# An expert's first and third matrix: one unit each with products of 256 columns, in place of halves of both with products of 512

## The reference

```python
def run(args):
    e, xb = args
    h = jax.nn.silu(xb @ w1[e]) * (xb @ w3[e])
    return h @ w2[e]
```

## Time and profile before

| | us |
|---|---|
| median of 3 runs | 2414.84 |
| lowest, highest | 2403.18, 2431.26 |
| the profiled execution | 2418.18 |
| its span, first to last instruction | 2416.5 |
| TensorE busy | 2115.9 (88%) |
| VectorE busy | 1528.7 (63%) |
| ScalarE busy | 1182.5 (49%) |
| mean granted TensorE clock | 0.871 |

### The profile page before, as it was taken

The page is one execution under the profiler, slowest core; times in us unless marked ns, Lnnn a source line. Parts: engine busy times, 40 slices in busy tenths (PEclk is TensorE's granted clock), DMA queues, the critical chain, the costliest instruction groups (busy, mean ns, idle before and its releaser), DMA issues.

```text
span 2416.5 us, 27567 instructions
## 1 busy us (share of the span) xinstructions
PE 2115.9 (88%) x9196; PEld 1693.5 (70%) x9196; DVE 1528.7 (63%) x1917; ACT 1182.5 (49%) x1407; POOL 124.9 (5%) x173
## 2 busy tenths in 40 slices
PE   5889989985899999999558899898859999999992
PEld 4776657864787788778447766677648877788871
DVE  4344344236699999999433443524258999999992
ACT  3333232222577777777332332423127777777771
POOL 0000000000010001001000000000000110000110
PEclk9885559997899999999778755899869999999996
DMA  6200022323799999999442000223239999999983
GB/s 223 102 3 0 1 86 72 101 99 122 265 365 362 367 366 369 372 365 365 154 156 104 1 1 1 105 87 114 92 132 341 368 361 369 363 362 368 371 327 119
DMA packets 148804, 501.40 MB, mean 207 GB/s; under 512 B 25312, under 2 KB 25312, under 8 KB 148704
## 3 DMA queue, kind: packets, MB, share of 16 engines
q1 hardware_dynamic: 135984, 460.80, 52.4%
q0 software_dynamic: 12720, 39.33, 4.4%
HBM read 484.35 MB, written 25.17 MB: 211 GB/s over the span
## 4 chain that ended last, share of the span: by engine, by line
PE 78%; DVE 9%; issue 5%; ACT 5%; DMA 2%; SPq 1%; DVEq 0%; POOL 0%; POOLq 0%; ACTq 0%
PE ps L1214 21%; PE ps L1216 20%; PE ps L1215 20%; PE ps L1393 4%; PE ps L1379 3%; PE ps L1351 3%; PE ps L1347 3%; DVE wl L852 1%; ACT wh L583 1%; PE ps L1483 1%; ACT whm L583 1%; PE ps L1442 1%; DVE sel L1129 1%; DMA y<-yrows 1%; PE ps L1455 1%
## 5 line engine op out<-in xcount | busy, mean ns | idle before, releaser
L852 DVE TENSOR_TENSOR wl<-raw,wh 128x2048 fp32r<-128x2048 f32 (+3 forms) x270 | 545.3, 2046 | 300.7 <-ACT wh L583 299.6
L583 ACT ACTIVATE wh<-raw 128x2048 fp32r<-128x2048 f32 (+3 forms) x270 | 455.4, 1718 | 286.9 <-PE ps L1216 277.5
L852 DVE TENSOR_TENSOR wlm<-raw,whm 128x2048 fp32r<-128x2048 f32 x192 | 436.2, 2288 | 52.7 <-ACT whm L583 52.7
L583 ACT ACTIVATE whm<-raw 128x2048 fp32r<-128x2048 f32 x192 | 362.6, 1908 | 0.0
L1214 PE MATMUL ps<-wh,xgh 128*128 128x512 f32 x520 | 212.0, 408 | 1.4 <-issue 1.4
L1216 PE MATMUL ps<-wh,xgl 128*128 128x512 f32 x520 | 207.7, 400 | 0.0
L1214 PE MATMUL ps<-whm,xgh 128*128 128x512 f32 x504 | 205.0, 407 | 2.5 <-DVE xgl L856 2.5
L1215 PE MATMUL ps<-wl,xgh 128*128 128x512 f32 x520 | 207.3, 399 | 0.0
L1216 PE MATMUL ps<-whm,xgl 128*128 128x512 f32 x504 | 197.1, 391 | 0.0
L1215 PE MATMUL ps<-wlm,xgh 128*128 128x512 f32 x504 | 196.7, 390 | 0.0
L767 ACT ACTIVATE hth<-ps 128x256 fp32r<-128x256 f32 x128 | 49.2, 384 | 192.2 <-PE ps L1483 192.2
(11 more groups left out here) (304 smaller groups left out, 3991.9 us busy)
## 6 DMA issues: line engine op xcount, KB each, us to landing
raw<-in_w SPq DMA_DIRECT2D x512, 512.0 KB
raw<-in_w SPq DMA_DIRECT2D x128, 1024.0 KB
raw<-in_w_gate SPq DMA_DIRECT2D x16, 1024.0 KB
x<-xres POOLq DMA_DIRECT2D x4, 2048.0 KB, 8.3
raw<-in_w_out SPq DMA_DIRECT2D x8, 1024.0 KB
raw<-in_w_in SPq DMA_DIRECT2D x8, 800.0 KB
raw<-in_w_oa SPq DMA_DIRECT2D x4, 1024.0 KB
raw<-in_w_ob SPq DMA_DIRECT2D x4, 1024.0 KB
```

The lines of the kernel that those rows point to most:

```text
L583: last = nc.scalar.activation(dst, src, ACT.Copy)
L852: last = V.tensor_tensor(dst, src, hi.bitcast(F32), ALU.subtract)
```

## The change

An up unit holds one whole matrix: half 0 is `w1` of the expert, half 1 is `w3`. SyncE loads it with one DMA of 1 MB, whose run is 8 KB for each partition, and the semaphore is raised by 32 at once. TensorE makes for each of the 8 values of k three products of 256 columns, into columns 0 to 255 (half 0) or 256 to 511 (half 1) of the same bank. As each up unit now reads all of `xgh` and `xgl`, both halves of the next block's tokens are split behind up(7,1), and the first up unit of a block waits for both. The wait of ScalarE for the unit ahead of `rows_hi` goes, as the sigmoid just ahead has the same one.

```diff
@@ load_units (SyncE)
-                            kh = KD // 2
-                            for j, w in enumerate((w1, w3)):
-                                src = w[l].rearrange("e (p k) f -> e p k f", k=KD)
-                                sp.dma_start(dst.rearrange("p (j k f) -> p j k f", j=2, k=kh)[:, j],
-                                             src[bass.ds(ex, 1), :, half * kh:(half + 1) * kh, :]
-                                             .rearrange("o p k f -> (o p) k f")).then_inc(got, 16)
+                            src = (w3 if half else w1)[l].rearrange("e (p k) f -> e p (k f)", k=KD)
+                            sp.dma_start(dst, src[bass.ds(ex, 1)].rearrange("o p n -> (o p) n")).then_inc(got, 32)
@@ act_block, step (ScalarE)
-                        if kind == "up" and e == NE - 1 and prepare:
-                            act.wait_ge(S["unit_used"], r * NU + (n + 1))
-                            rows_hi(b + 1, half)
+                        if kind == "up" and e == NE - 1 and half == 1 and prepare:
+                            rows_hi(b + 1, 0)
+                            rows_hi(b + 1, 1)
@@ dve_block, step (VectorE)
-                        if kind == "up" and e == NE - 1 and prepare:
-                            rows_lo(b + 1, half)
+                        if kind == "up" and e == NE - 1 and half == 1 and prepare:
+                            rows_lo(b + 1, 0)
+                            rows_lo(b + 1, 1)
@@ pe_block, up (TensorE)
                         if e == 0:
-                            pe.wait_ge(S["xgl_done"], b * 2 + (half + 1 + BASE["xgl_done"]))
+                            pe.wait_ge(S["xgl_done"], b * 2 + (2 + BASE["xgl_done"]))
                         if half == 0:
 
                             pe.wait_ge(S["hw_done"], b * (2 * NE) + (2 * (e - 1) + BASE["hw_done"]))
-                        kh = KD // 2
-                        for k in range(kh):
-                            kk = half * kh + k
-                            ww = [w.rearrange("p (j k f) -> p k j f", j=2, k=kh)[:, k]
-                                  for w in (hi_at(n), lo_at(n))]
-                            last = mm3(ps[e % 2][:, :], xgh[:, kk, :], xgl[:, kk, :], *ww, kk == 0, kk == KD - 1)
+                        for k in range(KD):
+                            ww = [w[:, k * FE:(k + 1) * FE] for w in (hi_at(n), lo_at(n))]
+                            last = mm3(ps[e % 2][:, half * FE:(half + 1) * FE], xgh[:, k, :], xgl[:, k, :], *ww,
+                                       k == 0, k == KD - 1)
                         last.then_inc(S["unit_used"], 1)
```

## The result

The changed kernel takes 2454.33 us (median of 16 runs, 2437.1 to 2470.42), the kernel before, run beside it, 2404.31 us (median of 16, 2398.61 to 2432.47). The ratio is 1.0172, 95% interval 1.0136 to 1.0208: slower by 1.7%. It is the ratio of the means of these runs, 2452.3 and 2410.9 us; the medians differ by 50 us, 2.1%. Ratios further down aren't ratios of two medians either, and leave out runs that lie far above the fastest of their kernel. Forecast were 2,455 us and 1.7% slower.

The account below looks back on a forecast made before the run. TensorE's issue of products was taken to bound the kernel. Products +32, turns +7 and layer heads +1.4 made +40 us on the profiled 2,418.2, so 2,458, or 2,455 us for the median, 1.7% slower; range 2,418 to 2,500.

Parts of the forecast that it names:

- The bound: Expert block: TensorE's issue of products sets the 70.19 us; the DMA keeps pace and ScalarE never waits for landed units.
- The products: Up units: 3,072 products of 512 columns become 6,144 of 256, 0.120 us apart in place of 0.2297 per 512: +32 us.
- the line through 384 and 512 columns: Product start distances 0.1765 and 0.2329 us, 0.441 ns a column, extended to give 0.120 us at 256 columns.
- The turn: Between blocks, the first product waits for both rows_lo: 0.5 us at each of 14 turns, +7 us, plus 1.4 at layer heads.
- the 0.1 deducted for a TensorE that comes later: At the block's turn, TensorE arrives 0.12 us later itself, so the 0.60 us delay was counted as 0.5.
- the head of the first stage: At each layer's first block, the first product waits for both rows_lo: +0.7 us, twice, 1.4 us.
- rival 5: Up units: each added weight load stands bare, costing 0.111 us in full, +341 us, 2,764 us in all; chance 0.02.
- 1 (columns alone, 0.115): Up products: the surplus goes with the columns, distance near 0.115 us, 2,423 us, within 1%; chance 0.20.
- 2 (load floor, 0.111): Up products: only the weight-load floor counts, distance 0.111 us, products gain 24 us, 2,399 us; chance 0.08.
- Rival 3: Up products: load and stream collide when equally long, distance 0.13 us or more, 2,516 us at 0.130; chance 0.09.
- rival 4: Up-unit loads: DMA becomes the bound with 8 KB runs; 2,476 us at a rate 5% lower; chance 0.03.

Follow-up runs that it names:

- the products alone: Kernel before with only each up product of 512 columns cut into two of 256, old loads and token-split order kept: 2450.55 us, ratio 1.0187.
- The order alone: Kernel before with only both halves of the next block's token split moved behind up(7,1), first product waiting for both: 2429.8 us, ratio 1.0101.

## Why the prediction was right

**The bound.** TensorE's distances set the block, not the DMA. The 8 KB runs changed the DMA share by 3 points and the block by nothing, and ScalarE's splits had no idle time ahead of them in either kernel.

**The products.** The step was 3,072 x (2 x 0.120 - 0.2297) = +32 us, and the distance of 0.120, read off the line through 384 and 512 columns, was measured. Its last digit is in part luck: both points of the line were of tile wh, the tiles differ by 7 ns at 512 columns and not at 256, and no run here explains the surplus. The term itself was too large. The run with the products alone gave 23.1 us (11.7 and 11.4), 8.5 less, and three things make up most of it. The mean distance of the up products before was nearer to 0.231 than to 0.2297 (92 distances in wh of 0.2333, 89 in whm of 0.2288), as whm units run their first products at the slower distance: 3,072 x 0.0014 = 4.3 us. Two waits for `hw` shrank, as a longer up unit gives VectorE time. Behind up(0,1) the transposes started 0.54 us after the last product had (839.09 to 839.63), 0.31 more than a product of 512 columns takes; in the run alone it is 0.27, 0.15 more than one of 256 takes. And the 0.15 us ahead of the turn went. Together 0.31 a block, 5 us in 16, and the prediction counted it nowhere, though the wait for `hw` stands in the earlier trace rows. In the other direction the down products of whm stood 0.2291 us apart in place of 0.2264, which took 1.9 us.

**The turn.** Forecast 14 x 0.5 + 1.4 = 8.4 us. The order alone cost 10.2 in its stages, 0.61 a block: the 0.60 that the prediction worked out from the length of rows_lo. It can't test the 0.1 deducted for a TensorE that comes later, since its products are the old ones. The changed kernel can, and there the deduction was right: rows_lo began 0.23 us behind the last down product before (897.21 to 897.44) and 0.08 after (744.49 to 744.57), so TensorE came 0.15 later, where 0.12 was forecast, and the stretch to the first product grew by 0.46. The same 0.15 is what the run with the products alone shows as a shorter wait; it must be counted once. At the head of the first stage the first product came 7.88 us behind the start of the gather (594.43 to 602.31) in place of 7.10 (611.17 to 618.27), +0.8 where 0.7 was forecast.

**The sum.** 40 us were forecast, 33.5 came in the stages: the mechanism was right, its size a fifth too large. That 2,455 us and 1.7% were met so closely is luck. The forecast stood on a median of three runs, 2414.84; with sixteen it is 2404.31, in the lowest step, while the changed kernel's median lies one step up. The means are 41 us apart, the medians 50.

**The rule on weight loads.** The prediction let the rule in the Trainium skill (TensorE: Matmul & The Clock Gate, Part 3, "The mechanism"), that a load overlaps a product in flight only when the row groups differ, stand as rival 5, 2,764 us. The traces don't agree: a product of 256 columns with its own full-height load takes 0.120 us, which leaves no room for a load of 0.111 that stands bare.

**The rivals.** Of 1 (columns alone, 0.115) and 2 (load floor, 0.111) neither distance came. Rival 3 wanted 0.13 us or more, and rival 4 a ScalarE that waits for landed units.

## What to carry to other kernels

Where each product brings its own weight load, a product's price here was its columns at 2.4 GHz and 13 to 20 ns, but never under 0.111 us, and a load hid only behind the one product ahead of it; so cut work into few long products, and take the distance from starts, not busy times. A change of layout that makes an operand whole needs its whole partner as well: look which small operation, split in halves until now, must be complete before the first product. What a profile names as the last wait can be an operation that ended by chance at that moment; a run without it settles that. And compare stages between two fixed events of the trace before believing a median whose runs stand in steps.

## What was not expected of the hardware

**Steps of the clock.** The runs of the two kernels stand in steps, of some 14 us before and some 16 after. The profiled runs show where: in the attention stages, whose instructions are the same in all. The same stretches of the kernel before (first layer, then second):

```profile
300.00:345.00 45.00, 41.08 (x141) 29.04 (x141) 14.77 (x35) 11.64 (x30) 0.76 (x1) 0.50 0.09 31
1510.00:1555.00 45.00, 33.13 (x168) 24.70 (x168) 23.61 (x41) 18.59 (x37) 0.76 (x1) 0.81 0.33 117
```

and of the changed kernel:

```profile
300.00:345.00 45.00, 33.10 (x166) 23.84 (x167) 25.21 (x44) 19.32 (x38) 0.76 (x1) 0.77 0.27 92
1510.00:1555.00 45.00, 36.31 (x126) 25.92 (x126) 18.34 (x41) 15.87 (x36) 0.76 (x1) 0.50 0.13 47
```

The granted clock (third number from the end) stays at 0.50 through this stretch in one layer and comes back within it in the other, and which layer it is differs between the two runs: 611 against 594 us ahead of the first expert stage, 616 against 633 ahead of the second. A layer that gets the clock early is 15 to 18 us shorter. How often a kernel gets it may depend on when its second layer begins: by its times the order alone got it in both layers in none of ten runs. That is read off counts and not shown; nothing here sets it.

**No surplus at half the clock.** In the first unit of a stage, at 1.2 GHz (granted clock 0.50), 512 columns of the kernel before stand 0.427 us apart (618.83 to 623.53, eleven distances), which is 512/1.2. In the changed kernel 256 columns stand 0.2133 us apart (603.73 to 605.65, nine distances), which is 256/1.2, but that number alone would prove little: products of 20 columns, each with its load, stand 0.213 us apart at this clock, so the load's floor is the same. The 13 to 20 ns come only at 2.4 GHz. Why 512 columns have 20 ns there with one tile and 13 with the other, while 256 have 13 with both, stays open.

**A jump back over a long body.** 6.5 and 7.2 us of TensorE at the two jumps of a loop with 960 products in its body, 0.3 to 0.4 with 576. The long body was also the one with two pairs of token tiles, and its cause stays open.
